# Up-projection chunks without overlap, and attention with turned probabilities as the stationary operand

## The reference

```python
def conv_ffn(x, w_up, w_dw, b_dw, w_down):
    h = depthwise_conv(x @ w_up, w_dw, b_dw)          # width 3, 2 * 2752 channels
    g, u = jnp.split(h, 2, axis=-1)
    return (jax.nn.silu(g) * u) @ w_down

def windowed_gqa(x, w_q, w_kv, w_o, sink):            # 16 heads of 64, 4 key/value heads
    ...
    m = jnp.maximum(jnp.max(scores, -1, keepdims=True), sink_l)
    p = jnp.exp(scores - m)
    probs = (p / (jnp.sum(p, -1, keepdims=True) + jnp.exp(sink_l - m))).astype(x.dtype)
    out = jnp.einsum('bngrqk,bnkgd->bnqgrd', probs, vb)
    return out.reshape(B, S, N_HEADS * HEAD_DIM) @ w_o
```

## Time and profile before

| what | value |
|---|---|
| median of three runs | 3077.22 us |
| the profiled execution, its own time | 3077.01 us |
| its span, first to last instruction | 3075.2 us |
| TensorE matmul busy | 2920.1 us (95%) |
| VectorE busy | 1681.1 us (55%) |
| ScalarE busy | 786.5 us (26%) |
| GpSimd busy | 986.1 us (32%) |
| mean granted TensorE clock | 0.976 |

### The profile page before, as it was taken

The page is one execution under the profiler, slowest core; times in us unless marked ns, Lnnn a source line. Parts: engine busy times, 40 slices in busy tenths (PEclk is TensorE's granted clock), DMA queues, the critical chain, the costliest instruction groups (busy, mean ns, idle before and its releaser), DMA issues.

```text
span 3075.2 us, 36198 instructions
## 1 busy us (share of the span) xinstructions
PE 2920.1 (95%) x14070; PEld 2386.1 (78%) x14070; DVE 1681.1 (55%) x2708; ACT 786.5 (26%) x1731; POOL 986.1 (32%) x817
## 2 busy tenths in 40 slices
PE   8999959889999999999899899898999999999996
PEld 7888847778888888888688544576788888888884
DVE  3689963674444444444720698666743444444447
ACT  3221342421111111112221466404211111111121
POOL 3355402362233223323131333224532233223323
PEclk9999979999999999999899899999999999999998
DMA  4000003111111111111121000211111111111111
GB/s 128 28 26 16 28 1 117 28 39 30 42 42 37 32 42 42 35 42 35 62 71 30 21 1 1 86 42 28 42 41 29 41 42 38 31 42 42 37 36 72
DMA packets 156950, 124.69 MB, mean 41 GB/s; under 512 B 27953, under 2 KB 133849, under 8 KB 156792
## 3 DMA queue, kind: packets, MB, share of 16 engines
q1 hardware_dynamic: 149736, 96.85, 11.2%
q10 hardware_dynamic: 7056, 25.69, 2.2%
HBM read 112.03 MB, written 10.49 MB: 40 GB/s over the span
## 4 chain that ended last, share of the span: by engine, by line
PE 85%; DVE 10%; ACT 4%; issue 1%; DMA 0%; POOL 0%; POOLq 0%; DVEq 0%; SPq 0%; ACTq 0%
PE bank L638 26%; PE bank L633 26%; PE bank L636 25%; PE bank L990 3%; PE bank L966 2%; DVE conv_acc L1356 2%; PE bank L981 1%; DVE stats L1286 1%; ACT y L1147 1%; PE bank L665 1%; ACT gained_tile L1035 1%; DVE y L1303 1%; DVE y L1305 1%; ACT probs L1236 1%; DVE y L1572 1%
## 5 line engine op out<-in xcount | busy, mean ns | idle before, releaser
L633 PE MATMUL bank<-x_hi,w_hi 128*128 128x498 f32 (+3 forms) x2688 | 962.1, 358 | 39.1 <-DVE up_conv L1480 18.1
L638 PE MATMUL bank<-x_hi,w_lo 128*128 128x498 f32 (+3 forms) x2688 | 962.7, 358 | 0.0
L636 PE MATMUL bank<-x_lo,w_hi 128*128 128x498 f32 (+3 forms) x2688 | 958.8, 357 | 0.0
L546 POOL CAST w_hi<-raw_pieces 128x512 fp32r<-128x512 f32 x348 | 341.9, 983 | 1750.2 <-issue 1253.3
L633 PEld LDWEIGHTS bank<-x_hi,w_hi 128*128 128x128 f32 x2688 | 508.8, 189 | 111.4 <-issue 30.2
L636 PEld LDWEIGHTS bank<-x_lo,w_hi 128*128 128x128 f32 x2688 | 507.4, 189 | 70.7
L638 PEld LDWEIGHTS bank<-x_hi,w_lo 128*128 128x128 f32 x2688 | 506.9, 189 | 69.4
L550 POOL TENSOR_TENSOR w_lo<-raw_pieces,w_hi 128x512 fp32r<-128x512 f32 x348 | 479.6, 1378 | 27.9
L1474 DVE SCALAR_TENSOR_TENSOR gate_conv<-bank,ffn_conv_table,gate_conv 128x496 f32<-128x496 f32 (+2 forms) x176 | 92.7, 547 | 613.5 <-ACT up_conv L1173 610.0
L1513 DVE TENSOR_TENSOR y<-y,bank 128x512 f32<-128x512 f32 x440 | 298.2, 685 | 225.4 <-PE bank L638 220.5
L1173 ACT ACTIVATE gate_conv<-bank,ffn_conv_table 128x497 f32<-128x497 f32 x132 | 93.6, 709 | 969.2 <-PE bank L638 969.2
(11 more groups left out here) (147 smaller groups left out, 3707.3 us busy)
## 6 DMA issues: line engine op xcount, KB each, us to landing
raw_pieces<-in_ffn_w_up_dram SPq DMA_DIRECT2D x168, 256.0 KB, 2.9
raw_pieces<-in_ffn_w_down_dram SPq DMA_DIRECT2D x84, 256.0 KB, 2.6
raw_pieces<-in_conv_w_pw_dram SPq DMA_DIRECT2D x48, 256.0 KB, 2.7
y<-in_x_prompt_dram ACTq DMA_DIRECT2D x16, 512.0 KB, 6.4
residual_dram<-y ACTq DMA_DIRECT2D x10, 512.0 KB, 2.7
y<-residual_dram ACTq DMA_DIRECT2D x10, 512.0 KB, 9.6
out_dram<-y SPq DMA_DIRECT2D x10, 512.0 KB, 2.6
raw_pieces<-in_attn_w_q_dram SPq DMA_DIRECT2D x32, 128.0 KB, 2.4
```

What stands on the lines that cost most here:

```text
L546: pool.tensor_copy(WH[:, p % RING, :], raw[:, p % RAW, :]).then_inc(piece_hi, 1)
L633: mm = pe.matmul(out, left[0], right[0], start=first, stop=False)
L636: pe.matmul(out, left[0], right[1], start=False, stop=False)
L638: return pe.matmul(out, left[1], right[0], start=False, stop=last)
```

## The change

Up-projection: the chunks become the 512, 512 and 256 columns of `CHUNKS`, without overlap. The outputs of a chunk are split differently: chunk 0 makes outputs 0 to 510, chunk 1 outputs 511 to 1023 (513 of them), chunk 2 outputs 1024 to 1279. Since chunk 1 no longer computes columns 510 and 511, ScalarE copies these two columns of gate and up to `edge_columns` while they are in the bank of chunk 0; in chunk 1 it makes the centre tap of output 511 from them, and VectorE adds their left taps to the first two outputs.

Attention: the probabilities are no longer normalised before the transposes. The turned probabilities become the stationary operand, 128x128 per head and key block, and V is streamed with 64 columns; the output of a unit then stands with queries on the partitions, and `keep_heads` divides it there by the denominator, one per partition and head. Four such units fill a query block, and `turn_heads` transposes it back in two halves, in TensorE's steps 4n + 4 and 4n + 6, into bank 7, which was the third score bank. Blocks 8 and 9 are turned inside the output projection. The turned probabilities have six buffers instead of two, in the columns of `x_hi` and `x_lo` of the sample. The maximum with the sink and the negation are one operation. GpSimd has no part in the attention any more. The residual of block n is loaded once its second half is turned.

```diff
-UP_CHUNKS = [(0, 498), (496, 498), (992, T - 992)]
-OUT_AT = [0, 497, 993, T]
-OUT_MAX = 497
+OUT_AT = [0, HALF - 1, S0, T]
+OUT_MAX = HALF + 1
...
+    edge = sb("edge_columns", [P, 2, 2], where=a)
...
-SCORE_BANKS = (0, 1, 7)
+UNIT_OF = [i for i, (n, _, _) in enumerate(ATT) for _ in key_blocks(n)]
+SCORE_BANKS = (0, 1)
+KEY_RING = 6
+TURNED_LATE = (TT - 2, TT - 1)
+def probs_turned_block(u):
+    v = u % KEY_RING
+    whole, k = (probsT_first, 2 * v) if v < KT // 2 else (probsT_last, 2 * v - KT)
+    return whole[:, k:k + 2, S0:S0 + 2 * P].rearrange("p k (r t) -> p k r t", t=P)
+def av_bank(i):
+    return bank[5 + i % 2][:, 0:GROUP * HD]
+def heads_step(i):
+    return [(n, half) for n in range(TT) if n not in TURNED_LATE for half in range(2)
+            if i == 4 * n + 4 + 2 * half]
...
-    for i in range(len(ATT)):
-        if i < RING - 1:
-            stretch(B_O + i, B_O + i + 1)
-        normalise_half(i)
-    stretch(B_O + RING - 1, B_FFN1)
+    ffn_stretch(B_O, B_FFN1)
...
-            for ch, (x0, n) in enumerate(UP_CHUNKS):
+            for ch, (x0, n) in enumerate(CHUNKS):
...
-            if u >= 3:
-                pe.wait_ge(score_kept, u - 2)
-            pe.matmul(bank[SCORE_BANKS[u % 3]][:, 0:len(kb) * P], q_sb[half, GROUP * rr + r, cols(n)],
+            if u >= 2:
+                pe.wait_ge(score_kept, u - 1)
+            pe.matmul(bank[SCORE_BANKS[u % 2]][:, 0:len(kb) * P], q_sb[half, n, GROUP * rr + r, :],
...
+    def turn_heads(n, half):
+        pe.wait_ge(heads_ready, 4 * n + 4)
+        if n or half:
+            pe.wait_ge(heads_lo, 2 * n + half)
+        for k in range(4):
+            mm = pe.transpose(bank[7][:, cols(k)], y[:, n, cols(4 * half + k)], ident[:])
+        mm.then_inc(heads_turned, 1)
...
             pe.wait_ge(probs_T_kept, KEYS_TO[i])
-        pe.wait_ge(probs_ready, i + 1)
-        pe.wait_ge(probs_ready_pool, i + 1)
+        pe.wait_ge(exp_ready, i + 1)
         for j in range(len(kb)):
...
             scores(i + 3)
+        for m, half in heads_step(i):
+            turn_heads(m, half)
         if i >= 2:
-            pe.wait_ge(av_lo, i - 1)
+            pe.wait_ge(heads_ready, i - 1)
         g = 2 * rr + par
-        for j, b in enumerate(kb):
-            pe.wait_ge(probs_T_kept, KEYS_TO[i] + j + 1)
-            pe.matmul(bank[5 + i % 2][0:HD, :], v_sb[:, b, g * HD:(g + 1) * HD],
-                      probsT[:, (KEYS_TO[i] + j) % 2, :], start=(j == 0), stop=(j == len(kb) - 1)
-                      ).then_inc(av_done, 1)
-    pe.wait_ge(av_lo, len(ATT))
-    out_projection(B_O, 1)
+        pe.wait_ge(probs_T_kept, KEYS_TO[i + 1])
+        for r in range(GROUP):
+            for j, b in enumerate(kb):
+                mm = pe.matmul(av_bank(i)[:, r * HD:(r + 1) * HD],
+                               probs_turned_block(KEYS_TO[i] + j)[:, r // 2, r % 2, :],
+                               v_sb[:, b, g * HD:(g + 1) * HD], start=(j == 0), stop=(j == len(kb) - 1))
+        mm.then_inc(av_done, 1)
+    late = [(n, half) for n in TURNED_LATE for half in range(2)]
+    pe.wait_ge(score_kept, GROUP * len(ATT))
+    out_projection(B_O, 1, lambda k: turn_heads(*late[k]) if k < len(late) else None, (heads_lo, 2 * TT))
     last_down = ffn(1, 3)
...
-            centre = OUT_AT[ch] - UP_CHUNKS[ch][0]
...
-                ins = act.activation(to[:, 0:n], bank[2 * (s % 2) + part][:, centre:centre + n], ACT.Identity,
+                source, first = bank[2 * (s % 2) + part], 1 if ch == 1 else 0
+                if ch == 0:
+                    act.activation(edge[:, part, :], source[:, HALF - 2:HALF], ACT.Copy).then_inc(ffn_edge, 1)
+                elif ch == 1:
+                    act.wait_ge(ffn_edge, 2 * (FT_ALL * layer + f) + part + 1 - layer)
+                    act.activation(to[:, 0:1], edge[:, part, 1:2], ACT.Identity,
+                                   scale=tab(1, part), bias=tab(3, part))
+                ins = act.activation(to[:, first:n], source[:, 0:n - first], ACT.Identity,
...
+    def heads_high(n, half):
+        act.wait_ge(heads_turned, 2 * n + half + 1)
+        act.activation(XH[:, 4 * half:4 * half + 4, cols(n)],
+                       bank[7][:].rearrange("p (k t) -> p k t", t=P), ACT.Copy).then_inc(heads_hi, 1)
+        if half:
+            act.dma_start(y[:, n, :], residual_rows[n]).then_inc(res_landed[n], 16)
...
-            if u >= 2:
-                act.wait_ge(av_done, u - 1)
-            act.activation(probsT[:, u % 2, :], bank[2 + j][:, :], ACT.Copy).then_inc(probs_T_kept, 1)
-        act.wait_ge(av_done, KEYS_TO[i + 1])
-        act.activation(XH[par * HD:(par + 1) * HD, GROUP * rr:GROUP * (rr + 1), cols(n)],
-                       bank[5 + i % 2][0:HD, :].rearrange("p (k t) -> p k t", t=P), ACT.Copy
-                       ).then_inc(av_hi, 1)
+            if u >= KEY_RING:
+                act.wait_ge(av_done, UNIT_OF[u - KEY_RING] + 1)
+            act.activation(probs_turned_block(u), bank[2 + j][:].rearrange("p (k r t) -> p k r t", k=2, t=P),
+                           ACT.Copy).then_inc(probs_T_kept, 1)
...
-    act.wait_ge(av_lo, len(ATT))
-    for t in range(TT):
-        act.dma_start(y[:, t, :], residual_rows[t]).then_inc(res_landed[t], 16)
+        for m, half in heads_step(i):
+            heads_high(m, half)
+    act.wait_ge(av_done, len(ATT))
+    for n in TURNED_LATE:
+        for half in range(2):
+            heads_high(n, half)
...
+                if ch == 1:
+                    dve.scalar_tensor_tensor(
+                        out=bufs[part][:, 0:2], in0=edge[:, part, :], scalar=tab(0, part),
+                        in1=bufs[part][:, 0:2], op0=ALU.mult, op1=ALU.add).then_inc(vec_step, vs.one())
...
-                dve.wait_ge(vec_step, vs.now() - (len(before) if f < FT and part == 0 else 0))
+                dve.wait_ge(vec_step, vs.now() - (len(before) + (ch == 1) if f < FT and part == 0 else 0))
...
             dve.scalar_tensor_tensor(out=probs[:, b, r, 0:nk], in0=dist[:, d0:d0 + nk],
-                                     scalar=-SLOPES[h0 + r], in1=bank[SCORE_BANKS[u % 3]][:, 0:nk],
+                                     scalar=-SLOPES[h0 + r], in1=bank[SCORE_BANKS[u % 2]][:, 0:nk],
                                      op0=ALU.mult, op1=ALU.add).then_inc(score_kept, 1)
...
         dve.wait_ge(vec_step, vs.now())
-        dve.tensor_tensor(nmax[:, b, :], nmax[:, b, :], sink[:, h0:h0 + GROUP], ALU.max
-                          ).then_inc(vec_step, vs.one())
-        dve.wait_ge(vec_step, vs.now())
-        dve.tensor_scalar(nmax[:, b, :], nmax[:, b, :], -1.0, None, ALU.mult).then_inc(vec_step, vs.one())
+        dve.scalar_tensor_tensor(out=nmax[:, b, :], in0=nmax[:, b, :], scalar=-1.0,
+                                 in1=nsink[:, h0:h0 + GROUP], op0=ALU.mult, op1=ALU.min
+                                 ).then_inc(vec_step, vs.one())
         dve.wait_ge(vec_step, vs.now())
...
-    def normalise(i):
-        n, rr, par = ATT[i]
-        nk, b = len(key_blocks(n)) * P, i % 3
+    def denominators(i):
+        b = i % 3
         dve.wait_ge(exp_ready, i + 1)
-        if i >= 3:
-            dve.wait_ge(probs_ready_pool, i - 2)
         dve.tensor_tensor(ssum[:, b, :], ssum[:, b, :], sexp[:, b, :], ALU.add).then_inc(vec_step, vs.one())
...
         dve.reciprocal(srec[:, b, :], ssum[:, b, :]).then_inc(recip_ready, 1)
+    def keep_heads(i):
+        n, rr, par = ATT[i]
+        dve.wait_ge(av_done, i + 1)
         dve.wait_ge(recip_ready, i + 1)
-        for r in range(GROUP // 2):
-            ins = dve.tensor_scalar(probs[:, b, r, 0:nk], probs[:, b, r, 0:nk], srec[:, b, r:r + 1],
-                                    None, ALU.mult)
-        ins.then_inc(probs_ready, 1)
-    def heads_low(i):
-        n, rr, par = ATT[i]
-        dve.wait_ge(av_hi, i + 1)
-        where = slice(par * HD, (par + 1) * HD), slice(GROUP * rr, GROUP * (rr + 1)), cols(n)
-        dve.tensor_tensor(XL[where], bank[5 + i % 2][0:HD, :].rearrange("p (k t) -> p k t", t=P),
-                          XH[where].bitcast(F32), ALU.subtract).then_inc(av_lo, 1)
+        dve.tensor_tensor(heads[:, n, GROUP * rr:GROUP * (rr + 1), par, :],
+                          av_bank(i).rearrange("p (r d) -> p r d", d=HD),
+                          srec[:, i % 3, :].unsqueeze(2).to_broadcast([P, GROUP, HD]), ALU.mult
+                          ).then_inc(heads_ready, 1)
+    def heads_low(n, half):
+        dve.wait_ge(heads_hi, 2 * n + half + 1)
+        where = slice(None), slice(4 * half, 4 * half + 4), cols(n)
+        dve.tensor_tensor(XL[where], bank[7][:].rearrange("p (k t) -> p k t", t=P),
+                          XH[where].bitcast(F32), ALU.subtract).then_inc(heads_lo, 1)
...
         biased_scores(i)
-    normalise(0)
+    denominators(0)
     for i in range(len(ATT)):
         if i + 1 < len(ATT):
-            normalise(i + 1)
+            denominators(i + 1)
         if i + 3 < len(ATT):
...
         if i >= 1:
-            heads_low(i - 1)
```

(22 more changed lines are left out.)

43 lines of the change are left out of this document (18 added, 25 removed).

## The result

Measured in turn with the kernel before on the same chip, the changed kernel takes a median of **3216.54 us** of six executions against 3077.47 us of six of the kernel before: a ratio of 1.045. Without the two longest executions (3225.69 and 3267.95 us, more than 1.5% above the shortest, which count as slow) the ratio is 1.041, with a 95% interval of 1.036 to 1.046. The prediction said 3105 us, 3074 to 3138. It is slower, as forecast, but by 139 us in place of 28, far outside the range. The six executions spread from 3177.72 to 3267.95 us, which no other kernel of this study does, and the spread follows TensorE's mean granted clock: 0.946 in the fastest, 0.930 at 3223.64 and 3225.69, 0.916 in the slowest. The slowest is the profiled one (span 3266.1 us), so its trace shows the effect at its largest; even the fastest is 100 us above the kernel before.

What follows compares the result with a forecast made beforehand. TensorE was taken as the bound, with 85% of the chain that ended last. Up-projection -25, attention +42 and clock +11 made +28 us on 3077.0, so 3105 us, range 3074 to 3138.

Steps and rivals of the forecast that it cites:

- (f): Attention: waits at the turn lower TensorE's granted clock, 8 x 1.4 = +11 us, bounds 0 and 27.
- Rival 4: Clock stays at 1.2 GHz for long stretches, small passes streaming half the time: 60 to 100 us more; chance 0.04.
- The up-projection: Short chunk falls from 6.39 to 5.75 us per 48 matmuls: -27.5 us, -25 after the give-back.
- Cost nothing: Up-projection tile change: the small border operations fit in the 2.1 us to spare, some 0.5 us left.
- the give-back of 2.6 us: Up-projection, tiles 0 and 1 of each layer: a shorter chunk only lengthens TensorE's wait for VectorE, 4 x 0.64.
- Rival 5: Up-projection: middle chunk's chain is late, some 40 tile changes wait 0.6 us or more; 3130 us, chance 0.06.
- (a): Attention, product with V: 24 passes of 64 columns at the load's pace, 2.8 us per unit, no change.
- rivals 1 and 2: Product with V: small passes cheap, 0.065 us each, 3068 (0.15); or load and stream in sequence, 0.16, 3147 (0.06).
- (b) to (e): Attention: turned heads +12 us, two score banks +5, wait at the turn +26, removed normalisation -1.5, +1.7 and -1.4.
- (c): Attention: with two score banks the third score waits for VectorE to empty the first, +0.2 x 24 = +5 us.
- (d): Attention: the turn of heads waits for the softmax front of scores just issued, eight waits, +26 us.
- rival 6: Attention: the turn does not wait because VectorE is far ahead; 3068 us, chance 0.03.

Runs made afterwards that it cites:

- wide_v: The changed kernel with the product with V on 128 moving columns in place of 64, half of each result unread: 3118.10 us (1.013).
- before_waits: The kernel before with one more TensorE wait, for VectorE's reduction of the scores, in eight attention steps: 3122.21 us (1.015).
- keep_early: The changed kernel with VectorE keeping the heads of unit i - 1 ahead of the denominators and biased scores: 3110.16 us (1.010).
- up_act: The kernel before with the change's up-projection alone, first column filled ahead of the matmul wait, border taps on ScalarE: 3053.39 us (0.992).
- up_only: The kernel before with the change's up-projection (chunks, tap columns, border operations) and the old attention: 3064.97 us (0.996).
- early_wide: The changed kernel with heads kept early and 128 moving columns in the product with V: 3080.75 us (1.0005).

## Why the prediction was wrong, step by step

**(f), the clock, is the step that failed.** "Scaled by the length of the wait, a wait of 3.3 us costs 1.4: 8 x 1.4 = +11 us", with an upper bound of 27. The price was taken from a fall among 512-column matmuls and used in a stretch with another stream. Where the stream is wide the step holds: 13 us in wide_v, 21 us in before_waits, both within its bounds. With passes of 64 columns it is 162 us in the profiled execution. The other executions have no trace; if all else in them is the same, it is an estimated 111 us at the median time and 72 in the fastest (162 less 51 and 90). Rival 4 named this mechanism, with 0.04: too small a chance. Its price of 60 to 100 us on top of the 11 was near for the median and too low for the slowest; two of the six executions lie in its 3165 to 3205 us. The chance left out how such passes raise a low clock, which the idle start of the attention and eight waits make necessary. A high clock they keep where TensorE has no wait (150 us of keep_early at 1.00), and not for certain behind short ones (the fall at 1957). The rule that the prediction weighed (the Trainium skill, TensorE: Matmul & The Clock Gate, A second HAM failure mode) says that frequent short idles make the clock go back and forth; wide_v and before_waits agree, with 13 and 21 us. The larger part is not a going back and forth: 235 us at 0.50 with TensorE busy for 95% of them.

**The up-projection**: the count was right (-27.5 forecast, 27.2 measured in up_act), what it meets was not. "Two one-column ScalarE operations and two two-column VectorE operations (at most 0.2 us each ...)" took 0.3 each and 0.19 and 0.71 in a later tile, and up to 2.29 in tile 0; what was left out is that VectorE waits for GpSimd in them. "Cost nothing" became 0.25 us at every second tile change, and the give-back of 2.6 us in the first tiles became 7 (the short chunk and the two long ones behind it take 41.4 and 43.1 us in the changed kernel, and 39.3 less 0.64 would be 38.7; up_act has 38.8 in the first layer): up_only gained 13.8 us, not 25. Rival 5 (0.6 us at every change) had the mechanism, at half the places and less than half the price.

**(a), the product with V**, was right in time: in keep_early at full clock 24 passes take 1844.39 - 1841.66 = 2.73 us, forecast 2.8, and in early_wide with 128 columns 2.79. A pass there costs what its load costs, so rivals 1 and 2 fall. These two rows of keep_early, timeline of PE, bound them:

```profile
1841.66 0.44 PE L1008 MATMUL bank<-v,probs_T_last 128*128 128x64 f32 x2
...
1844.39 1.48 PE L996 MATMUL bank<-ident,probs 128*128 128x128 f32 x12
```

**(b) to (e)** held. A turn of heads takes 0.49 us where 0.59 was said (1837.04 to 1837.53 in early_wide), the period of a unit without a turn is 7.30 us (1840.21 to 1847.51), that is +0.24 for (c), forecast +0.2. (d), the wait: 24.0 against 26; rival 6 falls. Without (d) and (f) the forecast's attention is 270.4 + 42 - 26 = 286 us, and early_wide's is 283.4.

Put together with what the runs showed: -14 + 13 (early_wide's attention against before) + 24 + 162 = +185 us, and the profiled execution stands at +191, the rest being the small stages of the table. With 13 in the place of 162, as with a wide stream, it would be +36, and wide_v is at +39.

What stays open is why the executions of the changed kernel differ by 90 us. That it goes with the granted clock is measured; what decides in which execution the clock comes back was not tried. Nor do the runs show why fewer moving columns keep it down: they show that they do.

## What to carry to other kernels

Price a fall of the clock by the stream that has to bring it back, not by the wait that caused it: the same eight 3 us waits cost 13 us of clock with 128 columns per stationary load and, in the profiled execution, 162 us with 64. Turning an operand so that it becomes stationary costs no time of its own when the load sets the pace, but a pass then streams for about half of its time, an estimated 0.06 us of 0.11 by the forecast's own working. Widening the stream with values that nobody reads cost 0.06 us per unit at full clock (2.79 against 2.73) and gave back 98 us. And an operation on two columns is not small when both its inputs are in SBUF while GpSimd reads there: keep such pieces off the engine that ends the chain.

## What was not expected of the hardware

A TensorE recorded as busy without a gap (25.00 of 25 us in keep_early) can be granted 1.2 GHz throughout; in the changed kernel that lasted for at least 235 us. In keep_early narrow passes lost the full clock behind a wait of 0.36 us; in early_wide, with waits of up to 0.31 us in the same units, wide ones kept it. An operation of VectorE on 128x2 in SBUF took 221 ns at its shortest and 2291 at its longest, and in each of the long ones it ended with one of GpSimd's:

```profile
L1511 DVE SCALAR_TENSOR_TENSOR gate_conv<-edge_columns,ffn_conv_table,gate_conv x44: 221/269/2291, 625.3 to 3176.7; 128x2 f32<-128x2 f32 x44
```

(Columns: shortest, median and longest ns, first and last start.) ScalarE's operation on one column held its queue for 0.3 us (0.3 between two starts), where 0.2 had been allowed as the most.
